# A decoder step on one core: the modulation with the condition as stationary operand, and cache pages stored in the order in which they are read

## The reference

```
def adaln(c, w, b, n):
    return jnp.split(jax.nn.silu(c) @ w + b, n, axis=-1)
```

```
def compress(rows, pe, w1, b1, w2):
    nc = (t - CMP_BLOCK) // CMP_STRIDE + 1
    idx = np.arange(nc)[:, None] * CMP_STRIDE + np.arange(CMP_BLOCK)[None, :]
    blocks = rows[:, idx] + pe[None, None, :, None, :]
    hid = gelu(einsum('bnlkd,ldh->bnkh', blocks, w1) + b1)
    return einsum('bnkh,hd->bnkd', hid, w2)
```

## Time and profile before

| | |
|---|---|
| median of 3 runs | 1512.8 us (1511.41 to 1526.06) |
| span of the profiled execution | 1510.7 us, 2.1 us under the median |
| PE busy | 1363.3 us (90%) |
| VectorE busy | 1016.6 us (67%) |
| ScalarE busy | 532.0 us (35%) |
| GpSimd busy | 301.0 us (20%) |
| share of the DMA engines' time, main queue | 38.9% |

### The profile page before, as it was taken

One profiled execution on the slowest core, in us unless ns is written; L12 is line 12 of the kernel. 1 busy time (PEld: TensorE's weight loads), 2 busy tenths in 40 slices (PEclk: granted clock), 3 DMA queues, 4 the chain that ended last, 5 costly groups with the idle time before them and its releaser, 6 DMA issues.

```text
span 1510.7 us, 25837 instructions
## 1 busy us (share of the span) xinstructions
PE 1363.3 (90%) x10092; PEld 912.0 (60%) x10092; DVE 1016.6 (67%) x1436; ACT 532.0 (35%) x1150; POOL 301.0 (20%) x301
## 2 busy tenths in 40 slices
PE   1789999999997879999987998999999988999996
PEld 1666666665554546666654766555766754666664
DVE  6899999969999477787347436653232346878634
ACT  2300100101101446666334231753222245666532
POOL 1275464635660001211001000000000000212000
PEclk9856656589998979999998995989788688999998
DMA  8646456364553303443451241003544421434340
GB/s 327 231 110 239 164 186 227 102 204 137 157 189 132 112 25 143 168 150 115 149 193 56 98 166 32 1 1 96 151 145 142 180 111 56 146 134 151 120 160 35
DMA packets 111051, 205.44 MB, mean 136 GB/s; under 512 B 71890, under 2 KB 96594, under 8 KB 100306
## 3 DMA queue, kind: packets, MB, share of 16 engines
q1 hardware_dynamic: 110930, 203.79, 38.9%
HBM read 199.39 MB, written 4.38 MB: 135 GB/s over the span
## 4 chain that ended last, share of the span: by engine, by line
PE 80%; DVE 12%; ACT 3%; issue 3%; DMA 1%; SPq 0%; DVEq 0%; ACTq 0%
PE PS L466 15%; PE PS L583 13%; PE PS L469 13%; PE PS L465 13%; PE PS L795 5%; DVE space L1212 4%; PE PS L743 4%; DVE wk_sb L1212 3%; PE PS L771 2%; PE PS L786 2%; PE PS L730 2%; PE PS L563 2%; PE PS L491 2%; PE PS L462 1%; ACT space L1066 1%
## 5 line engine op out<-in xcount | busy, mean ns | idle before, releaser
L465 PE MATMUL PS<-space_rounded 128*128 128x320 f32 x1344 | 567.5, 422 | 29.7 <-DVE space L1212 28.5
L466 PE MATMUL PS<-space_rounded,lo 128*128 128x320 bf16 x1344 | 428.7, 319 | 0.0
L469 PE MATMUL PS<-space,ring 128*128 128x320 bf16 x1344 | 404.6, 301 | 0.0
L1212 DVE TENSOR_TENSOR lo<-ring,space_rounded 128x1024 bf16<-128x1024 f32 (+1 forms) x172 | 206.0, 1200 | 246.1 <-ACT space_rounded L855 244.5
L465 PEld LDWEIGHTS PS<-space_rounded 128*128 128x128 f32 x1344 | 256.7, 191 | 101.0 <-DVE space L1212 39.5
L855 ACT ACTIVATE space_rounded<-ring 128x1024 fp32r<-128x1024 f32 (+1 forms) x172 | 177.0, 1033 | 253.7 <-PE PS L466 251.8
L583 PE MATMUL PS<-space 128*128 128x252 f32 x512 | 259.0, 652 | 0.0
L466 PEld LDWEIGHTS PS<-space_rounded,lo 128*128 128x128 bf16 x1344 | 130.0, 97 | 124.1 <-issue 7.9
L1212 DVE TENSOR_TENSOR lo<-ring 128x1024 bf16<-128x1024 f32 x112 | 169.3, 1521 | 18.0 <-PE PS L466 11.1
L583 PEld LDWEIGHTS PS<-space 128*128 128x128 f32 x512 | 118.0, 250 | 64.6 <-issue 49.2
L462 PE MATMUL PS<-silc,ring 128*128 128x9 bf16 x896 | 102.3, 171 | 43.2 <-DVE lo L1212 41.2
(11 more groups left out here) (189 smaller groups left out, 1922.1 us busy)
## 6 DMA issues: line engine op xcount, KB each, us to landing
ring<-w_mod SPq DMA_DIRECT2D x24, 2048.0 KB, 8.6
ring<-w_up SPq DMA_DIRECT2D x22, 2048.0 KB, 7.9
ring<-w_down SPq DMA_DIRECT2D x16, 1408.0 KB, 6.0
space<-pool_cmp SPq DMA_DIRECT2D x128, 128.0 KB, 2.6
ring<-w_mod_kv SPq DMA_DIRECT2D x4, 2048.0 KB, 10.2
ring<-pool_k SPq DMA_DIRECT2D x64, 128.0 KB, 2.4
ring<-pool_v SPq DMA_DIRECT2D x64, 128.0 KB, 2.1
ring<-w_kv SPq DMA_DIRECT2D x3, 2048.0 KB, 7.9
```

What stands on the lines that cost most here:

```text
L465: pe.matmul(out, wr[:, p % SPLIT, at:at + P], xr[:, k, :], start=start, stop=False)
L466: mm = pe.matmul(out, lo[:, p % SPLIT, at:at + P], xh[:, k, :], start=False, stop=False)
L469: return pe.matmul(out, w, xl[:, k, :], start=False, stop=stop)
L1212: return dve.tensor_tensor(out, a, b, op)
```

## The change

The two operands of the modulation change places. The condition `silu(c)`, padded with zeros from 9 to 32 columns, is the stationary operand, and the weights stream in fp32, with no split. A chunk is stored as 8 blocks of 128 x 512 (`_row_chunks`). Its 8 matmuls (`modulation_rows`) go to four strips of 32 output partitions: strip `g` sums blocks `2g` and `2g + 1`. So each strip holds a part of the 9 x 512 result. ScalarE copies the four strips from PSUM to `mod_rows` (one copy of 128 x 512 for each chunk). Four fp32 matmuls with these as the stationary operand and a 128 x 9 picking matrix as the moving one (`modulation_tiles`) add the strips and turn the result into the layout that `mod` had; the bias is added as before.

VectorE's `low_parts` for the modulation go (112 pieces), with their waits. The slots of the ring are free at `row_mm`, when the 8 matmuls are done. A unit's order on PE is: inputs, rows of the first chunk, half of the compression, tiles of the first chunk, the small compression step and the outputs of the unit before, rows of the second chunk, the other half, tiles of the second chunk.

The compressed pages are stored so that a page's 256 words of a partition lie in one piece in memory and in `XT`, and so that a matmul of the compression reads 8 runs of 32 neighbouring words. It has 256 columns in place of 252, and the two halves of `w1` write with an offset of 4 columns.

The core of the diff:

```
         for j in range(NMOD0):
-            add_chunk(f"mod{j}", whole(dram["w_mod"][j]), "mod_mm", j + 1)
+            add_chunk(f"mod{j}", whole(dram["w_mod"][j]), "row_mm", j + 1)
...
-                    sp.dma_start(XT[:, u % 2, :, 64 * j:64 * j + 64],
-                                 dram["pool_cmp"][e][page(NPG * b + j)].rearrange("p (h n) -> p h n", h=KVH)
-                                 ).then_inc(S(f"xt{u % 2}_in"), 16)
+                    sp.dma_start(XT[:, u % 2, j].rearrange("p r n -> p (r n)"),
+                                 dram["pool_cmp"][e][page(NPG * b + j)]).then_inc(S(f"xt{u % 2}_in"), 16)
...
+            def modulation_rows(j):
+
+                w = arrived(pe, f"mod{j}").rearrange("p (k n) -> p k n", k=KT)
+                if j >= 2:
+                    pe.wait_ge(S("mod_ev"), 4 * (j - 1) if j < NMOD0 else 4 * j)
+                for i in range(2):
+                    for g in range(4):
+                        k = 2 * g + i
+                        mm = pe.matmul(PS[32 * g:32 * g + 32, mod_bank[j], :], silc[:, k, :], w[:, k, :], start=(i == 0), stop=(i == 1))
+                mm.then_inc(S("row_mm"), 1)
+
+            def modulation_tiles(j):
+
+                pe.wait_ge(S("row_ev"), j + 1)
+                for m in range(4):
+                    mm = pe.matmul(PS[:, mod_bank[j], NB * m:NB * m + NB], mod_rows[:, j % 2, P * m:P * m + P], C["mod_pick"],
+                                   start=True, stop=True)
+                mm.then_inc(S("mod_mm"), 1)
...
-            pe.wait_ge(S("silb"), 2)
+            pe.wait_ge(S("silc"), 1)
+            pe.wait_ge(S("params_in"), 64)
             for j in range(NMOD0 - 1):
-                modulation(j)
+                modulation_rows(j)
+                modulation_tiles(j)
...
+            modulation_rows(NMOD0 - 1)
             sums(0)
-            modulation(NMOD0 - 1)
+            modulation_tiles(NMOD0 - 1)
...
-                    mm = pe.matmul(PS[:, 6, 0:KVH * NC], w1[:, l, :], XT[:, u % 2, :, l:l + 8 * (NC - 1) + 1:8],
-                                   start=(l == 0), stop=(l == 15))
+                    at = KVH if l < 8 else 0
+                    mm = pe.matmul(PS[:, 6, at:at + 256], w1[:, l, :], XT[:, u % 2, :, l % 8, :],
+                                   start=(l == 0), stop=(l == 15), skip_group_check=True)
...
-                modulation(mod_of_unit[u][0], between)
+                first, second = mod_of_unit[u][0], mod_of_unit[u][1:]
+                modulation_rows(first)
+                hidden_part(u, range(0, 8))
+                modulation_tiles(first)
                 if u >= 1:
                     compressed(u - 1)
                     outputs_of(u - 1)
-                for j in mod_of_unit[u][1:]:
-                    modulation(j, between)
+                for j in second:
+                    modulation_rows(j)
+                hidden_part(u, range(8, 16))
+                for j in second:
+                    modulation_tiles(j)
...
+            def modulation_rows(j):
+
+                act.wait_ge(S("row_mm"), j + 1)
+                if j >= 2:
+                    act.wait_ge(S("mod_mm"), j - 1)
+                act.activation(mod_rows[:, j % 2, :], bank(mod_bank[j]), ACT.Copy).then_inc(S("row_ev"), 1)
...
-            act.wait_ge(S("silc"), 1)
-            act.activation(silb[:, 0], silc, ACT.Copy).then_inc(S("silb"), 1)
...
+            pool.memset(silc_sb[:, :], 0.0).then_inc(S("eps"), 1)
...
-            dve.wait_ge(S("silb"), 1)
-            post(tt(silb[:, 1], silc, silb[:, 0], ALU.subtract), "silb", own=False)
...
-                low_parts(left[0])
+            dve.wait_ge(S("mod_mm"), 28)
             low_parts()
```

More of the change, by code:

```diff
@@ L45 @@
          ("causal", 2 * P), ("new_mask", DS), ("win_mask", DS), ("gate_pick", DS), ("cmp_valid", 2 * NCP),
-         ("cmp_neg", 2 * NCP), ("blocks", NFREE), ("scan_run", T), ("steps", 32)]
+         ("cmp_neg", 2 * NCP), ("blocks", NFREE), ("scan_run", T), ("steps", 32), ("mod_pick", NB)]
 VEC = [("norm_pre", 32), ("norm_post", 32), ("norm_kv", 8), ("b_mod", 112), ("ssm_d", 8), ("b_glu", 8),
@@ L273, in build_step @@
             for j in mod_of_unit[u]:
-                add_chunk(f"mod{j}", whole(mod_src[j]), "mod_mm", j + 1)
+                add_chunk(f"mod{j}", whole(mod_src[j]), "row_mm", j + 1)
         for j in range(2):
@@ L343, in build_step @@
         for name, loads, _, _ in stream:
-            if name[0:3] in ("mod", "glu") or name[0:2] in ("up", "kv") or name[0] in "qo" or name[0:4] == "down":
+            if name[0:3] == "glu" or name[0:2] in ("up", "kv") or name[0] in "qo" or name[0:4] == "down":
                 tiles = FT if name[0:4] == "down" else 32
@@ L460, in product @@
                 w = ring_hi[:, n % RING, P * tile:P * tile + P]
[L461 to L465, removed]
+                pe.matmul(out, wr[:, p % SPLIT, at:at + P], xr[:, k, :], start=start, stop=False)
                 mm = pe.matmul(out, lo[:, p % SPLIT, at:at + P], xh[:, k, :], start=False, stop=False)
@@ L969, in _ @@
                 hidden(u)
+                modulation_rows(mod_of_unit[u][0])
                 modulation(mod_of_unit[u][0])
@@ L1258, in low_parts @@
                         dve.wait_ge(S("lo_used"), p - SPLIT + 1)
[L1259 to L1262, removed]
+                    dve.wait_ge(S("hi_ready"), p + 1)
+                    high = wr[:, p % SPLIT, 0:cols].bitcast(F32)
                     post(tt(lo[:, p % SPLIT, 0:cols], ring[:, n % RING, c:c + cols], high, ALU.subtract), "lo_ready", own=False)
@@ L1404, in _ @@
                     post(ins, "bx_done")
-                    low_parts()
             for e in range(2):
@@ L1430, in _ @@
             modulated(0, 0, None)
-            low_parts(3)
             def cosine(s):
@@ L1448, in _ @@
                 v = VS[s]
[L1450 to L1455, removed]
                 dve.wait_ge(S("u_mm"), u + 1)
@@ L1650, in _weight_chunks, with _row_chunks @@
     return w.reshape(kt, P, mt // group, group, P).transpose(2, 1, 3, 0, 4).reshape(mt // group, P, group * kt * P)
+def _row_chunks(w):
+    K, M = w.shape
+    return w.reshape(K // P, P, M // 512, 512).transpose(2, 1, 0, 3).reshape(M // 512, P, K // P * 512)
 def _features(v):
@@ L1703, in _constants @@
     tab["steps"] = np.broadcast_to(np.concatenate([np.arange(16), 16 * np.arange(16)]).astype(f), (P, 32))
+    pick = np.zeros((P, NB), f)
+    for g in range(4):
+        pick[32 * g:32 * g + NB] = np.eye(NB, dtype=f)
+    tab["mod_pick"] = pick
     assert {n: t.shape[1] for n, t in tab.items()} == dict(CONST)
@@ L1757, in _lay_out @@
     wm = i["w_mod"].reshape(4, D, 3 * D)
-    d["w_mod"] = np.concatenate([_weight_chunks(wm[s], 4) for s in range(4)], 0)
-    d["w_mod_kv"] = _weight_chunks(i["w_mod_kv"], 4)
+    d["w_mod"] = np.concatenate([_row_chunks(wm[s]) for s in range(4)], 0)
+    d["w_mod_kv"] = _row_chunks(i["w_mod_kv"])
     d["w_glu"] = _weight_chunks(i["w_glu"][0], 4)
```

54 lines of the change are left out of this document (18 added, 36 removed).

## The result

The changed kernel takes 1384.9 us (median of 4 runs, 1378.69 to 1392.06) against 1512.7 of the kernel before on the same chip (four runs, three of which are in the table ahead of the prediction): ratio 0.9113, 95% interval 0.908 to 0.9146. That is 128 us less. The prediction was 110 us less, 1403, and its range began at 1386.

A forecast was written before the change was run, and what follows sets the result against it. PE and VectorE were both taken as full. Units 1 to 7 at 18.8 us (PE), unit 8 at 28.1, then units at 17.7 (VectorE) end the loop at 367.9, 110 us earlier: 1403 us, range 1386 to 1425.

The forecast's parts named there:

- the sum for PE of a unit with two chunks: PE in units 1 to 7: rows, tiles, compression, rest and allowances make 18.8 us a unit, before 27.3.
- Tiles: Four new fp32 matmuls a chunk on PE, 8 records at 0.219 us each, held up by weight loads: 1.75 us.
- nine changes between kinds: Switches between kinds of matmul on PE in a two-chunk unit, at 0.1 us each, bringing 17.1 to 18.0 us.
- the allowance for the half clock: 0.8 us added to PE's two-chunk unit for some matmuls at half clock, bringing 18.0 to 18.8 us.
- PE's stall at unit 8: Unit 8: load and bias as before, then 13.0 us, and 2.5 for half clock: 28.1 us.
- Rows: Row matmuls of a chunk on PE: four strips side by side, 4 steps, 1.74 us; high end 6.94.
- Compression: Compression on PE: 32 records a unit, 7.0 us instead of 14.7, if runs of 32 words read like long ones.
- VectorE: VectorE's unit without the `low_parts` pieces: 17.4 us, 17.7 with an addition, before 22.3; bounds one-chunk units.
- Clock: PE's clock after the change: above 0.9 of full speed from unit 1 on, as rows and compression stream without gaps.
- the rivals at half clock: PE stays at half clock: 1560 us, chance 0.03; a third of work there: 1455, chance 0.21 shared with program order.
- Start-up: Before unit 0: three chunks pass one by one; 4 us counted for unit 0's start at 61.3, bounds 0 and 8.
- ScalarE, transfers, new waits: ScalarE's 0.5 us copy a chunk hidden in the loop, pages in time by 3 us, new waits costing nothing.

The follow-up runs named there:

- e9: The changed kernel run again with nothing edited, on another chip; 1382.0 us, ratio 0.9055 to the kernel before.
- e7: The changed kernel with the tile matmuls of the modulation made twice for every chunk of the loop; 1391.4 us, ratio 0.9189 to the kernel before.
- e3: The changed kernel with all eight row matmuls of a chunk in one strip of 32 output partitions; 1495.3 us, ratio 0.9854 to the kernel before.
- e5: The changed kernel with the row matmuls issued strip by strip instead of turning through the strips; 1388.1 us, ratio 0.9165 to the kernel before.
- e1: The changed kernel with the old page layout, so only the new modulation; 1488.9 us, ratio 0.9809 to the kernel before.
- e6: The changed kernel with GpSimd's tables and decay left out from unit 2 on, so the output differs; 1359.6 us, ratio 0.8961 to the kernel before.
- e4: The changed kernel with the decay made by ScalarE instead of GpSimd, in two instructions; 1369.2 us, ratio 0.9034 to the kernel before.
- e8: The changed kernel with ScalarE making the decay, unit 1's early, and unit 8's rows, tiles and outputs ahead of PE's `cmp_w` wait; 1364.0 us.
- e10: The changed kernel with ScalarE making the decay, units 1 and 2 early, and unit 8's PE work ahead of its `cmp_w` wait; 1362.7 us.

## Why the prediction was right in sign and short in size

**The step that failed is the sum for PE of a unit with two chunks, 18.8 us; it takes 15.45.** Of the 3.35 us too many, 1.6 are the term "Tiles": 1.75 us a chunk, measured 0.95. It was taken from L574's 0.219 us a record, which ran at the half clock, and carried over as if the load of fp32 weights did not depend on the clock; it does, as the kernel after shows with 1.88 us at a granted clock of 0.50 and 0.95 at 1.00. The other 1.7 are the nine changes between kinds (0.9) and the allowance for the half clock (0.8). Neither is there: rows start beside outputs, and the clock is 0.97.

What hung on that step was larger than its size. At 18.8 PE would have been above VectorE's 17.4 and set the pace of units 1 to 7. At 15.45 it is below, and two things follow. VectorE, beside GpSimd, sets the pace of all fifteen distances, but for 2.1 us of waits. And PE runs ahead, by 1.9 us in a unit at the full clock: the inputs of unit 8 end at 197.60, and VectorE takes them up at 203.97. So PE's stall at unit 8, forecast at 28.1 us and measured at 25.14 from inputs to inputs, reaches VectorE only as a scan distance of 19.6, with 15.8 after it (two at VectorE's pace make 34.8), in e9 as 17.5. e7 is the test: with 1.9 us more a unit PE is at 17.1, and the stall shows again (23.9).

Against e9, whose start is the forecast one, the terms are: units 1 to 7, 131.6 forecast, 121.8 measured between scans (-9.8); unit 8, 28.1 against 17.5 (-10.6); unit 0 and units 9 to 15 together, with the lag from inputs to scan, 146.9 against 145.7 (-1.2). The sum is the 22 us by which its loop ends earlier than forecast. A forecast with 0.95 us for the tiles and without the two allowances, and so with VectorE in front from unit 1 to unit 8, would have stood at about 1382.

That the median lies only 1 us under the forecast range is in part luck. In the profiled executions the loop ended 29 us earlier than forecast (22 in e9), and the part behind it, forecast as unchanged, took 19 us more (9 in e9).

**The other steps.**

- *Rows*, 1.74 us a chunk: 1.85 measured. Four strips run wholly side by side (e3, e5). The Trainium skill, "TensorE: Matmul & The Clock Gate", Part 3, "The mechanism", has matmuls start strictly in program order. The trace disagrees: outputs that stand ahead of the rows start at 122.52, behind rows at 122.33, and in e5 all sixteen starts lie within 1.4 us.
- *Compression*, 7.0 us: two halves, 116.88 to 120.44 and 124.61 to 128.17, make 7.1. Right. e1 shows the old reading at 15 us and full clock, as the prediction had it.
- *VectorE*, 17.4 and 17.7: 17.3 and 17.5, right, and so is its reason: GpSimd's work now falls on the mixer's own steps (e6: 12.4 us alone). The Trainium skill, "SBUF — State Buffer", "SBUF: two separate sides", says that the port pair these two engines share is locked for a whole instruction. The trace agrees: GpSimd's product at 122.93 ends 0.90 us after the scan at 123.08 has begun, and that scan takes 3.58 us where it took 2.82.
- *Clock*, without a row in the prediction: 0.97 in units 1 to 7, as forecast (above 0.9), and the rivals at half clock are out.
- *Start-up*, 61.3: 61.15 in e9, 54.4 in the first profile. Right where three chunks have the half-clock lengths; the rest is when the clock rises.
- *ScalarE, transfers, new waits*, put at nothing: no idle time on VectorE in the loop hangs on them. The pages' 9.8 us became 8.14.
- *"What follows is left as it is"*: 1028.8 us before, 1037.4 and 1047.4 after. The attention holds most of the difference; its windows in the kernel before, after, and in e9:

```profile
920.70:1200.50 279.80, 253.22 (x1179) 179.02 (x1178) 114.20 (x286) 103.70 (x332) 0.00 (x0) 0.80 0.28 90
```

```profile
785.20:1080.20 295.00, 268.92 (x1179) 190.44 (x1178) 114.39 (x286) 103.95 (x332) 0.00 (x0) 0.75 0.28 85
```

```profile
791.40:1076.30 284.90, 257.94 (x1180) 185.20 (x1179) 114.32 (x286) 103.65 (x332) 0.00 (x0) 0.79 0.29 88
```

The same instructions, with clocks of 0.80, 0.75 and 0.79. The eleven profiles of the other kernels have 1033 to 1047 us behind the loop, and the one profile of before 1028.8; whether the change costs a few microseconds there, or that one profile was at the low end, stays open.

## What to carry over

When two engines are full, price the change as a pair: each half alone gave 26 us and nothing, both gave 128, because the pace falls only to the next engine's. When a duration is carried from one stage to another, carry its clock with it: a row measured at the half clock has a weight load doubled, as it has a stream doubled. And where two engines are forecast within 10% of each other, work out the sum with each of them in front, since the one behind also decides which stalls are covered.

## What had not been expected of the hardware

- Eight records with a 128 x 128 fp32 weight load and nine columns take 1.88 us at a granted clock of 0.50 and 0.95 at 1.00 (the kernel after, at 28.96 and 120.44).
- Four strips of fp32 matmuls with different data run side by side without loss in steps of 0.43 us for 512 columns, in whatever order they are issued (the kernel after and e5), and begin beside matmuls of another kind that are still running (122.33).
- The same instructions of the attention took 279.8, 295.0 and 284.9 us in three executions, with clocks of 0.80, 0.75 and 0.79. VectorE and ScalarE were as busy each time within 0.4 us, and PE's busy time took up the difference. That spread is nearly as large as what e4, e8 and e10 gained over the kernel after (16 to 22 us).
